# Seven half-size products in place of eight for the gate projections of a two-branch mixer, made ahead of the heads and kept in DRAM

## The reference, cut to what matters

```python
proj = h @ w_in                       # 1024 x 1024 by 1024 x D_IN
rq, rk, rv, rg, gq, gk, gv, gr, ga, gate_logits = split(proj)
# retention, 4 heads: q, k of 128 columns, v of 256; forward and backward scans, in chunks of 128 tokens
ret = norm(ret) * ret_norm * silu(rg)                   # rg: 4 heads x 256 columns
# gated linear attention (gla), 4 heads, decays from ga
gla = norm(gla) * gla_norm * silu(gr)                   # gr: 4 heads x 256 columns
g_ret, g_gla = split(sigmoid(gate_logits))              # 1024 columns each
merged = g_ret * (ret @ w_branch_ret) + g_gla * (gla @ w_branch_gla)
x = x + merged @ w_out
x = x + expert_choice_moe(rmsnorm(x))                   # 16 experts, unchanged
return rmsnorm(x)
```

## Time and profile before

| what | before |
|---|---|
| median of 3 runs (lowest, highest) | 2796.75 us (2796.71, 2798.09) |
| time of the profiled execution | 2797.05 us |
| its span in the profile | 2795.1 us |
| PE busy | 2702.9 us, 97% |
| DVE, ACT, POOL busy | 1916.0, 1617.9, 222.3 us |
| mean granted TensorE clock | 0.984 |

### The profile page before, as it was taken

One profiled execution on the slowest core, in us unless ns is written; L12 is line 12 of the kernel. 1 busy time (PEld: TensorE's weight loads), 2 busy tenths in 40 slices (PEclk: granted clock), 3 DMA queues, 4 the chain that ended last, 5 costly groups with the idle time before them and its releaser, 6 DMA issues.

```text
span 2795.1 us, 36818 instructions
## 1 busy us (share of the span) xinstructions
PE 2702.9 (97%) x13518; PEld 2322.2 (83%) x13518; DVE 1916.0 (69%) x1926; ACT 1617.9 (58%) x1479; POOL 222.3 (8%) x241
## 2 busy tenths in 40 slices
PE   7999999999999999957999999999999999999997
PEld 6888888888888888846888888888888888888886
DVE  6534425454564324367888888888888888888887
ACT  6232233353442322325777777787778778877786
POOL 0011010100101111000000000000000000000010
PEclk8999999999999999978999999999999999999998
DMA  4133351521525443357999999999999999999996
GB/s 121 49 98 71 66 97 36 104 76 54 103 53 132 86 103 107 134 218 264 373 385 377 391 374 385 379 388 372 383 379 390 372 385 376 391 372 384 378 392 278
DMA packets 253891, 689.96 MB, mean 247 GB/s; under 512 B 18444, under 2 KB 75916, under 8 KB 253808
## 3 DMA queue, kind: packets, MB, share of 16 engines
q1 hardware_dynamic: 227968, 622.01, 59.7%
q0 software_dynamic: 25840, 66.80, 10.9%
HBM read 634.22 MB, written 54.53 MB: 246 GB/s over the span
## 4 chain that ended last, share of the span: by engine, by line
PE 53%; DVE 2%; DMA 0%; issue 0%; ACT 0%; DVEq 0%; POOL 0%; POOLq 0%; ACTq 0%
PE e_gate_ps L2228 17%; PE e_up_ps L2228 17%; PE e_y_ps L2206 17%; PE e_turn L2182 1%; PE e_turn L2166 1%; DVE e_part L2035 0%; DVE e_top_at L2047 0%; DVE e_top L2046 0%; DMA e_xg<-h_mid,e_token_next 0%; DVE e_silu L2049 0%; DVE e_act L2049 0%; DVE e_raw L2088 0%; DMA out_dram<-e_raw 0%; ACT e_part L1955 0%; DVE e_xg L2142 0%
## 5 line engine op out<-in xcount | busy, mean ns | idle before, releaser
L2035 DVE TENSOR_TENSOR e_part<-e_raw,e_part 128x2048 fp32r<-128x2048 f32 (+2 forms) x576 | 1196.7, 2111 | 176.1 <-ACT e_part L1955 174.4
L1955 ACT ACTIVATE e_part<-e_raw 128x2048 fp32r<-128x2048 f32 (+2 forms) x576 | 1008.8, 1773 | 309.8 <-PE e_y_ps L2206 168.2
L105 PE MATMUL m_proj<-m_hT,m_w_part 128*128 128x512 f32 (+1 forms) x2352 | 557.1, 394 | 4.9 <-DVE m_hT L907 3.1
L105 PEld LDWEIGHTS m_proj<-m_hT,m_w_part 128*128 128x128 f32 (+1 forms) x2352 | 440.3, 188 | 98.5 <-DVE m_hT L907 3.7
L2206 PE MATMUL e_y_ps<-e_part,e_actT 128*128 128x512 f32 x2112 | 497.8, 392 | 0.1
L2228 PE MATMUL e_gate_ps<-e_part,e_xgT 128*128 128x512 f32 (+1 forms) x2304 | 496.1, 373 | 0.6 <-DVE e_xgT L2040 0.6
L2228 PE MATMUL e_up_ps<-e_part,e_xgT 128*128 128x512 f32 (+1 forms) x2304 | 489.0, 371 | 0.0
L2228 PEld LDWEIGHTS e_gate_ps<-e_part,e_xgT 128*128 128x128 f32 x2304 | 422.6, 188 | 61.8 <-issue 1.0
L2228 PEld LDWEIGHTS e_up_ps<-e_part,e_xgT 128*128 128x128 f32 x2304 | 421.6, 188 | 59.9
L2206 PEld LDWEIGHTS e_y_ps<-e_part,e_actT 128*128 128x128 f32 x2112 | 392.6, 188 | 79.8 <-issue 0.5
L887 DVE TENSOR_TENSOR m_w_part<-m_w_raw,m_w_part 128x1024 fp32r<-128x1024 f32 (+1 forms) x93 | 112.7, 1218 | 144.8 <-ACT m_w_part L550 144.8
(11 more groups left out here) (280 smaller groups left out, 1834.8 us busy)
## 6 DMA issues: line engine op xcount, KB each, us to landing
e_raw<-in_w_down_dram SPq DMA_DIRECT2D x160, 1024.0 KB, 7.3
e_raw<-in_w_gate_dram SPq DMA_DIRECT2D x128, 1024.0 KB, 7.8
e_raw<-in_w_up_dram SPq DMA_DIRECT2D x128, 1024.0 KB, 8.6
e_raw<-in_w_gate_dram SPq DMA_DIRECT2D x64, 768.0 KB, 8.9
e_raw<-in_w_up_dram SPq DMA_DIRECT2D x64, 768.0 KB, 6.1
m_w_raw<-in_w_in_dram SPq DMA_DIRECT2D x64, 512.0 KB, 4.7
ret_sum<-m_stage POOLq DMA_DIRECT2D x64, 256.0 KB, 4.7
gla_sum<-m_stage POOLq DMA_DIRECT2D x64, 256.0 KB, 4.7
```

The lines of the kernel that those rows point to most:

```text
L105: last = nc.tensor.matmul(out, x_at(x[xi], kc), w_at(w[wi], kc), start=start and kc == 0 and (xi, wi) == (0, 0), stop=stop and kc == chunk ...
L1955: nc.scalar.activation(part[k % PARTS][0][:, 0:size(k)], raw[k % RAW][:, 0:size(k)], ACT.Copy).then_inc(w_high, 1)
L2035: nc.vector.tensor_tensor(part[k % PARTS][1][:, 0:size(k)], raw[k % RAW][:, 0:size(k)], part[k % PARTS][0][:, 0:size(k)], ALU.subtract).th ...
```

## The change

The 12 groups of gate columns (8 heads' `C`, 1024 columns of `R`; a "pair" is 256 columns, that is two weight blocks) are projected ahead of all heads. Pair 0 is made as before (units `P`). The other 11 pairs are made by Strassen's scheme in Winograd's form: the weights of a pair and the transposed activations are cut in quarters, sums of quarters (`S1` to `S4`, `T1` to `T4`) are formed, and seven products of 12 matmuls (`multiply_pair`) are added up by DVE, where eight stood. The sums `T` of the activations are made once, in a rebuilt copy of the activations (`rebuild_x`, `make_t`); `T4` lies over a quarter of `hT` that is saved to DRAM and read back. The gates go to DRAM (`lit_gates`) and are read back four tiles at a time (`load_lit`). `L` moves to the start as well.

The heads lose their `C` units. Two of the next head's `A` units move behind `outputs`, in their place. `G` units 0 and 1 are made ahead of the last head's `E` units, and no unit stands between those.

```diff
     def middle_of(hd):
-        return [*s[0:2], fill[0], *s[2:4], fill[1], *s[4:6], fill[2], s[6], fill[3]]
+        a = [("A", hd + 1, i) for i in range(2)]
+        if hd == HD - 1:
+            return s
+        if is_ret(hd + 1):
+            return [*s[0:2], a[0], *s[2:5], a[1], *s[5:7]]
+        return [*s[0:2], a[0], *s[2:4], z[0], *s[4:6], a[1], z[1], s[6], *z[2:4]]
+    PAIRS = HD + 4
+    PRODUCTS = (("A11", "B11"), ("S2", "T2"), ("S3", "T3"), ("S1", "T1"), ("A12", "B21"), ("A22", "T4"), ("S4", "B22"))
...
# PE
+            for p in range(1, PAIRS):
+                multiply_pair(p)
             for i in range(4):
                 project_qk(0, i)
             for hd in range(HD):
                 nxt = hd + 1
+                project_v(hd, 0)
                 if hd:
-                    for t in range(6):
-                        branch(hd - 1, 2 * t)
-                        branch(hd - 1, 2 * t + 1)
-                        if t:
-                            project_v(hd, t - 1)
+                    flip(hd - 1, 2)
+                    flip(hd - 1, 3)
+                    project_v(hd, 1)
+                    for t in range(4):
+                        branch(hd - 1, t)
+                        project_v(hd, 2 + t)
...
+                    for i in range(8, 16):
+                        branch(hd - 1, i)
...
                 outputs(hd)
-                project_lit(("C", hd, 0))
-                project_lit(("C", hd, 1))
+                for i in range(2):
+                    if nxt < HD:
+                        project_qk(nxt, 2 + i)
+                    else:
+                        project_lit(("G", 0, i))
                 flip(hd, 0)
-                project_lit(("C", hd, 2))
                 flip(hd, 1)
-                flip(hd, 2)
-                project_lit(("C", hd, 3))
-                flip(hd, 3)
+            flip(HD - 1, 2)
+            flip(HD - 1, 3)
             for i in range(16):
+                branch(HD - 1, i)
+            for i in range(EARLY_G, 16):
                 project_lit(("G", 0, i))
+            def multiply_pair(p):
+                for k, (_, b) in enumerate(PRODUCTS):
...
+                    product(nc, quarter_bank(q), (0, 1), h, lambda i, kc: w[:, i * HALF + kc * P:i * HALF + (kc + 1) * P],
+                            lambda a, kc: a[:, kc, :], chunks=4).then_inc(multiplied, 1)
# ACT, start of a head
                 if hd:
-                    for u in range(12):
-                        take_sum(hd - 1, u)
...
+                    high_of_flip(hd - 1, 2)
+                    high_of_flip(hd - 1, 3)
+                    if gla:
+                        for k in range(2):
+                            for of_keys in range(2):
+                                exp_near(hd, k, of_keys)
+                    take_v(hd, 0)
+                    take_sum(hd - 1, 0)
+                    take_sum(hd - 1, 1)
# DVE, per pair of the new stage
+            for p in range(1, PAIRS):
+                more = p + 1 < PAIRS
+                if more:
+                    sums_of(p + 1)
+                    quarter_low_of(p + 1, 0)
+                else:
+                    split_low()
+                add_second(p)
...
# DVE, before the first head and at the end of each
             for w in range(2):
                 rope_first(w)
+            split_low()
...
+                if is_ret(nxt):
+                    rope(nxt, 2)
+                    rope(nxt, 3)
                 gate_flip(hd, 0)
+                gate_flip(hd, 1)
+                low_of_flip(hd, 0)
+                low_of_flip(hd, 1)
+                split_low()
                 if decays:
                     sum_gate(0)
# POOL
+            for hd in range(1, HD):
+                for u in range(8):
+                    add_sum(hd - 1, u)
+                for i in range(4):
+                    load_lit(nth_lit["C", hd, i])
+                for u in range(8, 16):
+                    add_sum(hd - 1, u)
...
             for u in range(16):
                 add_sum(HD - 1, u)
+                if u < 12:
+                    load_lit(nth_lit["R", 0, 4 + u])
```

More of the change, by code:

```diff
@@ L165, in mixer @@
         n_keys = 2 if is_ret(hd) else 4
         works += [("K", hd, i) for i in range(n_keys)] + [("Q", hd, i) for i in range(n_keys)]
-        middle = middle_of(hd)
-        works += [u for u in middle if u[0] in "SZ"] + [("F", hd, i) for i in range(4)]
-    TAIL = [("E", HD - 1, u) for u in range(4)] + [("R", 0, 4)]
-    for u in range(6):
-        TAIL += [("E", HD - 1, 4 + 2 * u), ("E", HD - 1, 5 + 2 * u), ("R", 0, 5 + u)]
-    TAIL += [("R", 0, u) for u in range(11, 16)]
-    units += TAIL
@@ L180, in mixer @@
+    units += [("G", 0, u) for u in range(2)] + [("E", HD - 1, u) for u in range(16)]
+    units += [("G", 0, u) for u in range(2, 16)]
     blocks += [("O", q, kb) for q in range(3) for kb in range(4)]
+    slot_of = [n if n < 3 else (n + 2) % SLOTS for n in range(len(blocks) - 4)]
+    slot_of += [SLOTS] + slot_of[-3:]
     works += [("X", t, 0) for t in range(2)]
@@ L187, in mixer @@
     nth_work = {u: n for n, u in enumerate(works)}
-    slot_of = [n % SLOTS for n in range(len(blocks) - 4)]
-    slot_of += [SLOTS] + slot_of[-3:]
     latest, freed_by = {}, []
@@ L194, in mixer @@
         latest[s] = n
-    lit = [u for u in units if u[0] in "CRG"]
+    lit = [("C", hd, i) for hd in range(HD) for i in range(4)] + [("R", 0, u) for u in range(16)]
+    FETCHED = len(lit)
+    EARLY_G = 2
+    lit += [("G", 0, u) for u in range(EARLY_G, 16)]
     nth_lit = {u: n for n, u in enumerate(lit)}
@@ L283, in mixer @@
         w_high = sem("w_high")
+        pair_in = [sem(f"pair_in{k}") for k in range(2)]
+        sums_made = sem("sums_made")
+        quarter_high = sem("quarter_high")
+        quarter_low = sem("quarter_low")
+        x_kept = sem("x_kept")
+        x_rebuilt = sem("x_rebuilt")
+        t_made = sem("t_made")
+        t_high = sem("t_high")
+        t_low = sem("t_low")
+        quarter_saved = sem("quarter_saved")
+        quarter_back = sem("quarter_back")
+        multiplied = sem("multiplied")
+        first_copied = sem("first_copied")
+        added = sem("added")
+        lit_made = sem("lit_made")
+        lit_stored = [sem(f"lit_stored{k}") for k in range(4)]
+        lit_in, LIT_IN = lit_stored, 16 * PAIRS
         w_split = sem("w_split")
@@ L312, in mixer @@
         r_in = [sem(f"r_in{j}") for j in range(KC)]
-        g_in = [sem(f"g_in{s}") for s in range(4)]
+        g_in, G_IN = lit_in, LIT_IN + 16 * (FETCHED // 4)
         gated = sem("gated")
@@ L325, in mixer @@
         mid_taken = sem("mid_taken")
-        res_in = [sem(f"res_in{t}") for t in range(NT)]
+        res_in = r_in
         row_in = sem("row_in")
@@ L384, in wait_slot_free @@
             kind, hd, i = blocks[freed_by[n]]
+            if 3 <= n < 6:
+                uses = [q for q in range(QUARTERS * (PAIRS - 1))
+                        if q % len(half_slots) in {0: (0, 1), 1: (2, 3), 2: (8, 9)}[slot_of[n]]]
+                eng.wait_ge(multiplied, uses[-1] + 1)
+                return
             if kind == "A":
@@ L476, in _ @@
                 sp.dma_start(ffn_gain[:], norm_ffn[0].rearrange("(c p) -> p c", p=P)).then_inc(small_in, 16)
-            for n in range(2, len(blocks)):
+            load(2)
+            load_pair(1)
+            load_pair(2)
+            load_pair(3)
+            sp.wait_ge(t_low, 4)
+            sp.dma_start(pos_i[:], positions.to_broadcast([P, SEQ])).then_inc(table_in, 16)
+            for p in range(4, PAIRS):
+                load_pair(p)
+            for n in range(3, 5):
+                load(n)
+            for n in range(5, len(blocks)):
                 load(n)
@@ L1165, in _ @@
             split_low()
+            rebuild_x(0)
             root_of_x(3)
```

661 lines of the change are left out of this document (469 added, 192 removed).

## The result

| | before | changed |
|---|---|---|
| median of 6 runs (lowest, highest) | 2797.06 us (2796.08, 2798.09) | 2877.41 us (2874.01, 2878.45) |
| ratio, 95% interval | | 1.0285 [1.0272, 1.0298] |
| span of the profiled execution | 2795.1 us | 2876.4 us |
| PE busy | 2702.9 us | 2713.3 us |
| PE idle (span less busy) | 92.2 us | 163.1 us |

The changed kernel is 80.4 us slower. I had said 39.8 us slower, with 2858 as the upper end. The sign was right, the size was half of what came. (One execution of a later kernel, the one with the gate loads behind the sums, took 6451 us; it stands in no ratio, and that kernel's median, 2847.7 us, would be 2847.3 without it.)

The account below looks back on a forecast made before the run. PE was taken to bound the kernel, other engines hidden behind its projections. Added waits and clock, stated as 69.7 us, less 29.9 saved gave +39.8, so 2836 us; 2822 to 2848 for the sum itself, 2806 to 2858 over all cases.

Parts of the forecast that it names:

- The gain: New stage: eleven pairs save 132 matmuls of PE's work, 29.9 us.
- The new stage at no wait: New stage: PE needs 19.1 us a pair, DVE at most 12.4, ACT 7.2, so PE never waits.
- The first value tile: Start of head 0: PE waits 6.9 us for DVE's split of the second value block, plus 2.5 for clock.
- Middles: Middles of heads: waits of 5.5 us ahead of three retention heads, 19.2 ahead of four gla heads, 2.5 in the last.
- Ends of heads: Ends of heads: 2.5 us for flips in retention heads, 12.4 behind exponentials in four gla heads, 2.1 in the last.
- Runs of `E`: Eight to ten `E` units in a row wait for sums: 2.5 us in three retention heads, 1 in four gla, 11.5.
- the ring: Runs of `E` units: four buffers of sums need a round of 6.6 us, with 5.8 us landing, against 5.44.
- The tail: After the last head: sixteen `E` units in a row wait 2.5 us (1 to 6), then `G` 2.9 (0 to 5).
- The sum of the waits: Whole mixer: all added waits, with 2.5 us for clock and the old tail's wait taken off, stated as 69.7 us.
- The clock: Matmuls after PE idles run at 1.2 GHz: priced at 2.5 us (0 to 3), behind the first value tile's wait only.
- the rival: Gla heads: each of eight 3 us pauses costs 2.5 us more at the 1.2 GHz level, 2856 us; chance 0.10.
- The rival of the sums' queue: Heads and tail: gate loads delay sums, +8.5 us in heads, +3.5 and +2 in tail, late read-back, 2854; chance 0.12.

Follow-up runs that it names:

- The best kernel: Changed kernel with `E` units spread, DVE's split between the ropes, reordered middles, last head's splits moved and six early `G` units in the tail: 2780.0 us, ratio 0.9938.
- the new middles: Against the changed kernel, middles of heads that a gla head follows run S S A S S S Z Z A S S Z Z: 2860.6 us.

## Why the prediction was wrong, point by point

- **The gain, 29.9 us.** Right: 2.72 us a product in the trace, 29.3 us when it is given back.
- **The new stage at no wait.** Right: 209.7 of 209.7 us busy. At the start, for which I had taken 1 us less waiting, there were 2.9 less.
- **The first value tile, 6.9 us and 2.5 for the clock behind it.** Right: 6.88 us, and 25.24 - 23.26 = 2.0. Here I did price the clock. The fault was to do it here alone.
- **Middles.** Small waits, somewhat too dear: 1.28 us ahead of `outputs` in three retention heads, 3.8 against 5.5; 3.5 to 4.0 us in four gla middles, 15.0 against 19.2; 1.06 against 2.5 in the last head.
- **Ends of heads.** Three flips at 0.34, 1.0 against 2.5; the exponentials' wait 2.64 four times, 10.6 against 12.4; the last head's flips and first `E` 2.0 against 2.1.
- **Runs of `E`, 11.5 us: mis-sized.** 15.0 us in the retention heads and 11.3 in the gla heads, 26.3 in all, above my upper bound of 20. I had the ring and the gate loads in the text, but took a value near the lower end "since scores spread their units"; scores are 0.5 us, a value tile 2.9. And I took the landing, 5.8 us, as a constant from a kernel in which the sums came in pairs. In the run the median was hardly higher (5.1 us against 4.7 before, 345 to 1060 us), but the slowest took 10.5 us against 8.4, and a run of `E` waits for its slowest. The gate loads are shown to be part of that: with them behind the sums the slowest took 8.1. What the weight blocks add was not tested.
- **The tail, 2.5 and 2.9 us.** 7.6 us for the sums, 2.3 for `G`. The same error in the first.
- **The sum of the waits.** The terms as they stand add up to 67.7 us, not to 69.7: 65.2 of waits and 2.5 of clock. The forecast that follows from them is 2834, 2 us further off. 65.2 us of waits against 70.9 us more idle time measured: the mis-sizings nearly cancel, which is luck and says little for the single terms.
- **The clock: the step that failed.** The sum priced slow matmuls behind one pause, 2.5 us, and put them at nothing behind all others. Of the 42.6 us by which the terms fall short, 40.3 - 2.5 = 37.8 are PE's busy time. Most of that is its own work getting slower: laid over PE's rows, the clock records of the two traces have PE busy at the 1.2 GHz level for 19.7 us before and 81.9 us after, and half of the difference, 31 us, is lost by it. The row that I held against the rival, a pause of 1.78 us with nothing behind it, is true and is seen again here (1.57 us, then 3.01). But my sum itself foresaw pauses of about 3 us in every gla head, and nothing in the trace of before had shown one of that length to be free; the only rows with PE idle for long, showed 0.50. I priced the rival for eight pauses, 20 us. There were sixteen: four ahead of the third `E` unit, four at `Z`, six in the heads' runs, two in the tail (3.60 and 2.32 us). The Trainium skill's rule, page "TensorE: Matmul & The Clock Gate", section "Why this matters for your kernels", to leave no idle gaps between bursts of matmuls, is borne out by this trace: 0.96 over the heads with the gaps, 1.00 with the same gaps filled.
- **The rival of the sums' queue**, 2854, named the right cause for the runs and tail, and the right size for its own part; it lacked the clock. Both rivals together would have given about 2874. I had treated them as alternatives, though a longer wait for a sum is just what makes the clock fall.

The other 9 us of the 40.3 are mostly no slow work. A row's end lies a little past the start of the next, so each unbroken stretch of matmuls is shown somewhat too long, and the wait behind it too short: a single `E` unit between two waits is shown with 1.63 us, where six matmuls in a row take 1.36. The changed kernel has 77 such stretches for 29 before. By the lengths of their last rows I estimate 8 us, which belong to the waits. The best kernel, with 47 stretches, is 5 us above 2673 (2702.9 - 29.9), 4 of them by the same estimate. With the pauses filled busy time was 16 us above 2673; 9 are accounted for in this way, some 3 by the tail's slow matmuls, and the rest stays open.

## What to carry to other kernels

A wait of PE can have two prices: those of up to 1.6 us cost their own length here, those of 2.6 to 4 us nearly always that and some 2 us more, since the matmuls behind them ran at 1.2 GHz, and those around 2.4 us did so about every other time. So break a long wait into short ones (the new middles) or put work into it if it can't be removed. When short units that need a transfer each are moved together, read the landing time under the load that they will then make, not in the kernel where they stood apart. And when work is made cheaper by moving it away, count what it had covered: here 29.9 us of matmuls were saved, and 110 us of waits and clock appeared, of which all but some 13 could be had back by other covers.

## What I had not expected of the hardware

- 210 more matmuls made the kernel 22.5 us faster. In the pauses they cost nothing, and they gave back 24 us of matmul time.
- Shortening a pause from 6.88 to 2.29 us changed the slow matmuls behind it by only 0.5 us (25.24 to 24.75; 23.26 without a pause) in three kernels, and by the whole 2 us in a fourth (23.26). Near 2.4 us it is mostly whether the price is paid that varies, so two kernels can differ by some us, as those with the gate loads moved and with the sums stored do, through pauses that both have alike.
- Four loads of 256 KB among sixteen adding transfers of 256 KB took the slowest of these from 7.4 us to 10.5 us to land (runs of head 2, loads behind and loads among them).
